# A decoder layer on one core: the output projection as seven block products in place of eight

## What is computed

```python
merged = g_nsa * (o_nsa @ w_branch_nsa) + g_sgu * (o_sgu @ w_branch_sgu)
mix = merged @ w_out                       # 512 x 1024 by 1024 x 1024
h = layer_norm(2 ** 0.25 * h + mix, ln1_g, ln1_b)
ffn = (silu(h @ w_ffn_gate) * (h @ w_ffn_up)) @ w_ffn_down
h = layer_norm(2 ** 0.25 * h + ffn, ln2_g, ln2_b)
```

## Time and profile before

| what | us |
|---|---|
| median of 3 runs (713.21 to 713.55) | 713.54 |
| the profiled execution's own time | 713.21 |
| its span in the trace | 711.5 |
| PE busy | 700.4 |
| DVE busy | 567.5 |
| ACT busy | 352.0 |

### The profile page before, as it was taken

How to read it: one execution, slowest core, us unless ns; L and a number is a source line. 1 busy time by engine, 2 the same in 40 slices (tenths; PEclk the granted TensorE clock), 3 DMA queues, 4 the chain that set the end, 5 groups by cost and what they waited for, 6 DMA issues and landing times.

```text
span 711.5 us, 11496 instructions
## 1 busy us (share of the span) xinstructions
PE 700.4 (98%) x4232; PEld 622.9 (88%) x4232; DVE 567.5 (80%) x918; ACT 352.0 (49%) x552; POOL 151.2 (21%) x167
## 2 busy tenths in 40 slices
PE   8999999999999999999999999999999999999995
PEld 7888988878888988888899899999999998888884
DVE  6885499787788785675889598999898886977877
ACT  6462777457777778222534244444544344145600
POOL 2942970422132210000000222222222210000001
PEclk9999999999999999999999999999999999999998
DMA  9612343111101205536532133233223328400102
GB/s 314 229 45 67 112 119 119 60 59 60 41 20 60 59 1 161 195 119 236 148 90 67 52 119 110 67 118 118 80 96 118 118 78 306 185 23 0 60 31 88
DMA packets 55716, 73.84 MB, mean 104 GB/s; under 512 B 4096, under 2 KB 40704, under 8 KB 55552
## 3 DMA queue, kind: packets, MB, share of 16 engines
q1 hardware_dynamic: 55392, 72.19, 30.6%
q0 software_dynamic: 144, 1.05, 0.7%
q10 hardware_dynamic: 144, 0.13, 0.1%
HBM read 70.21 MB, written 2.10 MB: 102 GB/s over the span
## 4 chain that ended last, share of the span: by engine, by line
PE 96%; DVE 2%; DMA 0%; ACT 0%; issue 0%; DVEq 0%; SPq 0%; ACTq 0%
PE ps L1981 65%; PE ps L2430 10%; PE ps L2064 5%; PE ps L2448 5%; PE ps L1993 4%; PE ps L1989 3%; PE ps L1990 3%; PE ps L2003 1%; PE ps L2421 0%; DMA stage<-in_w_in 0%; DVE ptl L1252 0%; PE ps L2164 0%; PE ps L2165 0%; DVE wl L1252 0%; DVE prob L1533 0%
## 5 line engine op out<-in xcount | busy, mean ns | idle before, releaser
L1981 PE MATMUL ps<-xh,wh 128*128 128x256 f32 (+1 forms) x416 | 135.0, 325 | 0.0
L1981 PE MATMUL ps<-xh,wl 128*128 128x256 f32 (+1 forms) x416 | 131.7, 317 | 0.0
L1981 PE MATMUL ps<-xl,wh 128*128 128x256 f32 (+1 forms) x416 | 131.6, 316 | 0.0
L1981 PE MATMUL ps<-ath,wh 128*128 128x256 f32 (+1 forms) x280 | 86.1, 307 | 0.0
L1981 PE MATMUL ps<-ath,wl 128*128 128x256 f32 (+1 forms) x280 | 86.0, 307 | 0.0
L1981 PE MATMUL ps<-atl,wh 128*128 128x256 f32 (+1 forms) x280 | 86.0, 307 | 0.0
L1981 PEld LDWEIGHTS ps<-xh,wl 128*128 128x128 f32 x416 | 79.3, 191 | 5.4
L1981 PEld LDWEIGHTS ps<-xh,wh 128*128 128x128 f32 x416 | 79.5, 191 | 3.1
L1981 PEld LDWEIGHTS ps<-xl,wh 128*128 128x128 f32 x416 | 79.5, 191 | 3.1
L1252 DVE TENSOR_TENSOR wl<-stage,wh 128x512 fp32r<-128x512 f32 (+2 forms) x73 | 64.6, 897 | 4.9 <-ACT wh L796 2.8
L1242 DVE TENSOR_TENSOR wl<-stage,wh 128x2048 fp32r<-128x2048 f32 (+1 forms) x19 | 43.1, 2267 | 27.8 <-ACT wh L793 19.6
(11 more groups left out here) (374 smaller groups left out, 1741.4 us busy)
## 6 DMA issues: line engine op xcount, KB each, us to landing
stage<-in_w_ffn_gate SPq DMA_DIRECT2D x22, 512.0 KB, 4.5
stage<-in_w_ffn_up SPq DMA_DIRECT2D x22, 512.0 KB, 4.5
stage<-in_w_in SPq DMA_DIRECT2D x20, 512.0 KB, 4.1
stage<-in_w_ffn_down SPq DMA_DIRECT2D x14, 512.0 KB, 4.2
quad_raw<-in_w_in SPq DMA_DIRECT2D x8, 512.0 KB, 9.4
stage<-in_w_out SPq DMA_DIRECT2D x8, 512.0 KB, 4.6
quad_raw<-in_w_ffn_down SPq DMA_DIRECT2D x4, 1024.0 KB, 10.1
arena<-in_x_t SPq DMA_DIRECT2D x8, 256.0 KB, 5.5
```

The costliest lines, as they stand in the source:

```text
L1981: return pe.matmul(out, (sh, sh, sl)[i], (mh, ml, mh)[i], start=start and i == 0, stop=stop and i == 2)
```

## The change

Tokens and channels of merged and rows and columns of `w_out` are halved, and the product of the 2 x 2 blocks is made of seven block products in place of eight. One block product is 256 tokens by 512 channels by 512 columns: 24 matmuls of 512 columns. Sums of blocks take the place of the eighth:

- Of merged, four sums (`s1` to `s4`, 128 x 1024 each), made by DVE from the strips, then split on ACT (`out_s_hi`) and DVE (`out_s_lo`) into places of `xh` and `xl` whose blocks are done with.
- Of `w_out`, sums of two, three and four blocks. They are made by transfers that add: POOL issues `w_out` blocks from memory with `accum_op=ALU.add` onto a block that already lies in SBUF (`more_rows`). `t_sums` is such a running sum; a plain copy `t_3` of it is kept after the first addition. The lo part of two of the seven weight operands, and of the first FFN unit, is made the way of `second_l`: ACT negates, a POOL transfer adds.
- The products run in the order 0 to 6. Product 0 is first taken out to SBUF by ACT (`first_product`), then products 3 and 5 accumulate onto its banks 0 and 1; product 4 accumulates onto the banks 4 and 5 of product 2. DVE adds results to `y` in ten steps (`take`), where before it had eight.
- Right column half of tiles 0 and 1 is done after product 4, and these two tiles are normalised then. Tiles 2 and 3 are done after product 6, whose halves stand around the transpose of tile 1.
- SP brings the residual and the first `w_out` block before the last branch unit, and the four loads for the layer normalisation wait for `s4` as well.
- The loops over the branch rounds on DVE and ACT are written out, without registers.

```diff
+        def merged(half, k_half):
+            return x_block(merge, half, k_half)
+        def spare(at):
+            return arena[:, at:at + 1024].rearrange("p (k n) -> p k n", n=256)
+        t_sums, b_21 = arena[:, 8192:10240], arena[:, 4096:6144]
+        t_3 = fact[:, 18:22, :].rearrange("p f n -> p (f n)")
+        first_product = arena[:, 4096:5120].rearrange("p (m n) -> p m n", m=2)
+        M_S = {"s1": spare(6144), "s2": spare(7168), "s3": s1,
+               "s4": spare(5120)}
+        M_S_AT = {"s1": (1, 0), "s2": (0, 0), "s4": (0, 1), "s3": (1, 0)}
+        M_SLOT = ([(wh[:, b, :], wl[:, b, :]) for b in range(2)] +
+                  [(ath[:, 2048:4096], atl[:, 2048:4096])] +
+                  [tuple(t[:, :, :].rearrange("p a b -> p (a b)") for t in (oth, otl))])
+        def m_slot(i):
+            return [t.rearrange("p (k n) -> p k n", k=4) for t in M_SLOT[i]]
...
+            def out_rows(dst, k_half, half, q):
+                to = dst.rearrange("p (k n) -> p k n", k=4)
+                for i in range(2):
+                    k = 4 * k_half + 2 * i
+                    sp.dma_start(to[:, 2 * i:2 * i + 2, :],
+                                 wout_d[:, k:k + 2, 512 * half:512 * half + 512]).then_inc(raw_arrived[q], 16)
+            sp.wait_ge(st_done, 4)
+            out_rows(t_sums, 1, 1, 0)
             sp.wait_ge(o_end, PAIRS)
             sp.dma_start(y[:, :, :], x_d).then_inc(x2_arrived, 16)
-            with sp.Fori(0, 2) as c:
-                for kh in range(2):
-                    load(2 * c + U_OUT + kh, kh, rows4(wout_d, kh, kh, 512 * c, 512))
+            load(U_BRANCH + 3, 1, rows4(sgu_d, 1, 0, 512, 512))
+            sp.wait_ge(w_lo, U_BRANCH + 3)
+            out_rows(stage[0][:, :], 0, 0, 2)
+            sp.wait_ge(more_in, 16)
+            for i in range(2):
+                part = slice(1024 * i, 1024 * i + 1024)
+                sp.dma_start(t_3[:, part], t_sums[:, part]).then_inc(raw_arrived[1], 16)
+            sp.wait_ge(mg_ok, 4)
+            out_rows(b_21, 1, 0, 3)
+            load(U_FFN + 1, 1, rows8(up_d, 1, 0))
+            sp.wait_ge(part_lo, 12)
+            load(U_FFN, 0, rows8(gate_d, 0, 0))
+            sp.wait_ge(s_sum, 8)
             sp.wait_ge(mg_lo, KD)
...
+            def more(n, dst, src):
+                if n > 1:
+                    pool.wait_ge(more_in, 16 * (n - 1))
+                pool.dma_start(dst, src, accum_op=ALU.add).then_inc(more_in, 16)
+            def more_rows(n, dst, k_half, half):
+                more(n, dst.rearrange("p (k n) -> p k n", k=4),
+                     wout_d[:, 4 * k_half:4 * k_half + 4, 512 * half:512 * half + 512])
+            pool.wait_ge(part_lo, 9)
+            more_rows(1, t_sums, 0, 1)
+            pool.wait_ge(raw_arrived[1], 64)
+            more_rows(2, t_sums, 0, 0)
+            pool.wait_ge(part_lo, 10)
+            pool.dma_start(stage[0][:, :].rearrange("p (k n) -> p k n", k=4), wout_d[:, 0:4, 512:1024],
+                           accum_op=ALU.add).then_inc(second_in, 16)
             pool.wait_ge(second_neg, 1)
+            more(3, M_SLOT[1][1], t_sums)
+            pool.wait_ge(part_hi, 13)
+            more_rows(4, t_sums, 1, 0)
+            pool.wait_ge(second_neg, 2)
+            more(5, M_SLOT[1][1], t_sums)
+            pool.wait_ge(second_neg, 3)
+            pool.dma_start(first_l[:, :], stage[0][:, :], accum_op=ALU.add).then_inc(second_in, 16)
+            pool.wait_ge(second_in, 32)
+            pool.wait_ge(w_hi, U_FFN + 1)
+            pool.memset(scrap[:, :], 0.0).then_inc(w_lo, 1)
...
+            late_split(U_BRANCH + 2, 0)
+            out_t_hi(2, t_sums, arrived_in=(0, 64))
+            for f in range(4):
+                merged_hi(f)
+            late_split(U_BRANCH + 3, 1)
+            act.wait_ge(w_used, U_BRANCH + 3)
+            out_t_hi(0, stage[0][:, :], arrived_in=(2, 64))
+            out_t_hi(3, b_21, arrived_in=(3, 64))
+            for f in range(4, 7):
+                merged_hi(f)
+            act.wait_ge(more_in, 32)
+            act.wait_ge(w_used, U_BRANCH + 4)
+            negated(M_SLOT[1][1], t_sums)
+            merged_hi(7)
+            out_s_hi("s1", 6)
+            act.wait_ge(in_used, 8)
+            act.wait_ge(second_in, 16)
+            act.copy(M_SLOT[0][0], stage[0][:, :]).then_inc(part_hi, 1)
+            act.copy(first_product, ps[:, 0:2, :]).then_inc(bank_out, 1)
+            out_t_hi(1, t_sums, 2)
+            out_s_hi("s2", 7)
+            out_s_hi("s4", 8, 9)
+            act.wait_ge(in_used, 10)
+            out_s_hi("s3", 5)
+            out_t_hi(0, t_3, arrived_in=(1, 64))
+            act.wait_ge(more_in, 64)
+            act.wait_ge(in_used, 11)
+            negated(M_SLOT[1][1], t_sums)
+            out_t_hi(1, t_sums, 4)
...
+            negated(first_l[:, :], stage[0][:, :])
+            split_to(first_h[:, :], U_FFN, 0, U_FFN)
+            root(1)
             act.wait_ge(w_arrived[1], arrived(U_FFN + 1)[1])
-            act.mul(second_l[:, :], stage[1][:, :], -1.0).then_inc(second_neg, 1)
+            negated(second_l[:, :], stage[1][:, :])
+            ht_hi_of(0)
...
+            def merged_sum(c, f):
+                gated(c, f, 1)
+                dve.wait_ge(br_prod, 8 * c + 4 + f + 1)
+                gn = merge[:, 4 * c + f, :]
+                dve.tensor_tensor(gn, gn, merge[:, 4 * c + f + 8, :], ALU.add).then_inc(mg_ok, 1)
+            def merged_lo(f):
+                dve.wait_ge(mg_hi, f + 1)
+                lo(xl[:, f, :], merge[:, f, :], xh[:, f, :]).then_inc(mg_lo, 1)
...
+            split(U_BRANCH + 2, 0)
+            out_t_lo(2, t_sums, 9)
+            for f in range(4):
+                merged_sum(0, f)
+                merged_lo(f)
+            dve.wait_ge(mg_ok, 4)
+            out_s(5, "s3", merged(0, 0), merged(1, 0))
+            split(U_BRANCH + 3, 1)
+            dve.wait_ge(sig_ok, 4)
+            for f in range(3):
+                gated(1, f, 0)
+            out_t_lo(0, stage[0][:, :], 10)
+            gated(1, 3, 0)
+            out_t_lo(3, b_21, 11)
+            for f in range(3):
+                merged_sum(1, f)
+                merged_lo(4 + f)
+            merged_sum(1, 3)
+            dve.wait_ge(mg_ok, KD)
+            out_s(6, "s1", merged(1, 0), merged(1, 1))
+            merged_lo(7)
+            out_s_lo("s1", 13)
+            out_t_lo(0, stage[0][:, :], 12)
+            out_s(7, "s2", M_S["s1"], merged(0, 0))
+            dve.wait_ge(s_sum, 7)
+            dve.tensor_tensor(M_S["s4"], merged(0, 1), M_S["s2"], ALU.add).then_inc(s_sum, 1)
+            out_s_lo("s2", 14)
...
+            take(5, 0, 0, b_banks, ALU.add, True)
+            dve.wait_ge(bank_out, 5)
+            take(6, 0, 0, first_product, ALU.add)
+            out_s_lo("s4", 15)
+            dve.wait_ge(in_used, 10)
+            take(7, 2, 1, c_banks, ALU.add, True)
+            out_s_lo("s3", 16)
+            out_t_lo(0, t_3, 14)
+            dve.wait_ge(in_used, 11)
+            take(8, 0, 1, a_banks, ALU.subtract, True)
+            for m in range(2):
+                moments(m, 0)
+            dve.wait_ge(ln_arrived, 64)
+            for m in range(2):
+                if m:
+                    dve.wait_ge(in_used, 12)
                 else:
-                    dve.wait_ge(w_used, U_OUT + 2)
-                add_rows(m, 0, m).then_inc(mg_lo, 1)
-                dve.wait_ge(mg_lo, KD + m + 1)
-                moments(m, 0)
-            split(U_OUT + 3, 1)
-            split_to(first_l[:, :], first_h[:, :], U_FFN, 0)
-            dve.wait_ge(ln_arrived, 64)
-            for m in range(MT):
-                if m < 3:
-                    dve.wait_ge(rows_done, 12 + m + 1)
-                else:
-                    dve.wait_ge(w_used, U_FFN)
-                add_rows(m, 1, m).then_inc(mg_lo, 1)
-                dve.wait_ge(mg_lo, KD + MT + m + 1)
+                    dve.wait_ge(rows_done, 10)
+                take(9 + m, m, 1, ps[:, 4 + m:5 + m, :], ALU.add)
+                dve.wait_ge(in_out, 9 + m)
                 step(moments(m, 1))
                 variance(m)
                 norm(m)
-                if m == 1:
-                    ht_lo_of(0)
+            dve.wait_ge(in_used, 13)
+            take(11, 2, 1, a_banks, ALU.subtract)
+            take(12, 2, 0, a_banks, ALU.add, True)
+            ht_lo_of(0)
+            ht_lo_of(1)
+            dve.wait_ge(in_out, 11)
+            for m in (2, 3):
+                moments(m, 1)
+            for m in (2, 3):
+                if m == 3:
+                    dve.wait_ge(in_used, 14)
+                else:
+                    dve.wait_ge(rows_done, 11)
+                take(11 + m, m, 0, ps[:, m:m + 1, :], ALU.add)
+                dve.wait_ge(in_out, 11 + m)
+                step(moments(m, 0))
+                variance(m)
+                norm(m)
...
+            pe.wait_ge(mg_lo, 4)
+            pe.wait_ge(br_prod, 12)
+            pe.wait_ge(part_lo, 10)
```

(28 more changed lines are left out.)

176 lines of the change are left out of this document (87 added, 89 removed).

## The result

The changed kernel is slower by 0.8%: 719.66 us against 713.55 us, medians of six runs each, ratio 1.0080 (95% interval 1.0063 to 1.0098). That is +6.1 us, where +4.5 was forecast (718.0, range 712.0 to 722.5). The profiled execution of the changed kernel has a span of 717.4 us, against 711.5 before. The changed kernel also spreads more: its six executions lie from 717.4 to 721.3 us, those of before from 713.2 to 714.8.

What follows compares the result with a forecast made beforehand. PE bounds the kernel, 96% of the chain. Terms: -5.44 us removed, +4.6 DVE ahead of tile 2, +2.8 transfers and ACT, +2.5 clock, together +4.5: 718.0 us on the median 713.54, range 712.0 to 722.5.

Steps and rivals of the forecast that it cites:

- The place and the meeting point: Tile 2's transpose on PE, at 364.48 us before; PE would idle 3.6 us ahead of it, waiting for DVE.
- DVE's sum: DVE's passes from 287.87 us to tile 1's normalisation: 64.8 us, ending at 352.7; ready for the layer normalisation at 342.5.
- The loads of the layer normalisation: Loads ahead of tile 0's take on DVE: data there at 344.5 us, making DVE 2.0 us late.
- The sharing of 16 engines: Fourth adding transfer and SP's plain loads share 16 engines: 13.4 us from about 329.5 to 342.9.
- The work of an adding transfer: Each adding transfer of 1 MB on POOL's queue: 5.0 us of work, bounds 2.8 and 8.0.
- The rival built on free overlap (-0.8 or +1.7): Transfers overlap with loads: -0.8 us if the clock holds (chance 0.12), +1.7 if it falls (chance 0.22).
- ACT's queue: On ACT, root(1) stands behind the negation and copy of the FFN unit, which wait for a load: +0.8 us.
- The clock: PE's clock falls in the 3.6 us wait ahead of tile 2's transpose: +2.5 us, bounds 0 and 2.5.
- What would show it: Expected trace signs on PE, DVE and POOL, among them 8 to 10 us from issue to landing for transfer four.
- The value of the removed matmuls: 24 matmuls fewer on PE in the output projection: 5.44 us less, gone but for 0.8 at tile 2's transpose.

Runs made afterwards that it cites:

- e4_plain: Changed kernel with the four adding transfers of w_out blocks from memory made plain copies, leaving those sums out; 714.41 us, ratio 1.0017 to the kernel before.
- e2_root_ln: Changed kernel with layer normalisation loads issued ahead of the gate load, and root(0) with its table load moved earlier on ACT; 717.58 us, ratio 1.0056.
- e1_fill: Changed kernel with 26 transposes of the identity added on PE ahead of tile 2's transpose; 718.23 us, ratio 1.0072 to the kernel before.
- e9_root3: e6_all with ACT's copy of the next gate weights moved behind root(3); 711.03 us, ratio 0.9976 to the kernel before.
- e3_gate_late: e2_root_ln with the gate load issued only once the fourth adding transfer has landed; 718.01 us, ratio 1.0060 to the kernel before.
- e8_before_less: Kernel before the change with 24 matmuls of 512 columns left out of the output projection, nothing added; 710.17 us, ratio 0.9952.
- e11_root3_plain: e9_root3 with the four adding transfers from memory made plain copies, leaving those sums out; 710.32 us, ratio 0.9956 to the kernel before.
- e6_all: Changed kernel with e2_root_ln's and e12_tile2's edits, DVE strips interleaved, a gating moved earlier, and t_sums copied earlier on ACT; 716.97 us, ratio 1.0048.
- e12_tile2: Changed kernel with only tile 2's part of take 12 and the moments ahead of tile 2's normalisation on DVE; 718.36 us, ratio 1.0071.
- e7_all_fill: e6_all with 18 transposes of the identity added on PE ahead of tile 2's; 716.22 us, ratio 1.0040 to the kernel before.
- e10_root3_fill: e9_root3 with 18 transposes of the identity added on PE ahead of tile 2's; 711.26 us, ratio 0.9968 to the kernel before.

## Why the prediction was right, point by point

- **The place and the meeting point** were right: tile 2's transpose, with a gap of 3.24 us ahead of it (3.6 forecast), ended by DVE.
- **DVE's sum** was 1 us too high: the two moments ahead of tile 0 ended at 341.5 (340.21 and 1.28 in the timeline), where the sum had 342.5. Of this 0.6 goes with the projection, which started that much earlier (315.39 in the trace, 316.1 in the sum). The strips took 2.70 each, for 2.75.
- **The loads of the layer normalisation** were forecast for 344.5 and the take behind them ran at 344.19. DVE's wait for them was 2.71 us, for 2.0, because DVE came 1 us earlier than in the sum and not because they came later. The sharing of 16 engines is borne out: from 338 to 342 us POOL's queue had 58.6% of them and SP's 50.0%. The Trainium skill, "DMA: Bandwidth & Descriptors", section "Issuing engines are not separate DMA queues", says that transfers of different issuing engines interleave on the same 16 engines, and the trace agrees.
- **The work of an adding transfer** was nearly right: 5.0 us, where the eight of the changed kernel took 5.6 each. The fit in the Trainium skill, "DMA: Bandwidth & Descriptors", section "Anatomy of one DMA — SWDGE (gpsimd) path", gives an estimate of 4.4 us to landing for 1 MB; the plain one of e4_plain that ran with little beside it took 5.3, those that add from 7.0 to 14.4. For these the measurement decides. The rival built on free overlap (-0.8 or +1.7) fell with it.
- **The term that was mis-sized is ACT's queue**, +0.8 for `root(1)`. It was `root(0)` that came late, by 1.87 us: ahead of it stood not only the negation but the copy and a table load of 1.28 us, all behind the fourth transfer. `root(1)`, for which the sum had the 0.8, kept DVE waiting for nothing here (0.84 us in e2_root_ln). These 1.07 us more, less 0.3 for the loads, and some 0.2 in DVE's passes put tile 2's transposes at 367.51 in the trace, where 366.5 was forecast: 1.0 us. The ledger shows 1.8 (+3.8, for +2.0), since it counts from a projection that started 0.6 us earlier, and the transposes of before stand at 364.32 in the timeline where the chain has 364.48.
- **The clock** was right: +2.6 in the profile, 2.5 forecast, and e1_fill shows the cause. The 2.5 was the upper bound of the term; the clock fell behind each gap of 3.1 us or more in these profiles, but behind 2.66 us (e9_root3) the executions went both ways, so with a shorter gap the same reasoning would have been a matter of luck. A second fall, at 352 to 356 us after a gap of 1.82 us ahead of tile 0, I had not foreseen; it slowed half of product 6 and was hidden but for about 0.2 us: from tile 0's to tile 1's transposes it is 5.33 us, and 5.11 in e1_fill, whose clock held there. In e2_root_ln and e3_gate_late the same fall was not hidden.
- **What would show it** named 8 to 10 us for the fourth transfer, against the prediction's own sum, which had 13.4 for all that shares. It took 14.4.
- **The value of the removed matmuls**, 5.44 "gone but for 0.8", was not the limit of the idea: e9_root3 gets 2.2 us of it and e8_before_less, with nothing added, 3.2.

## What to carry to other kernels

Matmuls taken away pay only as far as the engine that feeds the next dependent matmul has slack; look at the first transpose or product behind the saving, count everything that stands ahead of it on every engine, in queue order, and count a gap in PE twice, once as waiting and once as lost clock. A sum made by an adding transfer is not free because POOL is idle: it holds all 16 engines for 5.0 to 5.6 us per MB, so it delays the plain loads beside it, and what waits for it in an in-order queue (here a negation on ACT) delays the small operations behind it. A short operation on the path, such as a square root, belongs ahead of a long one that waits for a transfer, and its table can be loaded in idle time before.

## What the runs showed of the hardware that was not expected

An adding transfer from memory, alone in the stretch 293 to 297 us of the changed kernel:

```profile
DMA packets 385, 0.79 MB, mean 197 GB/s; under 512 B 0, under 2 KB 0, under 8 KB 385
...
q0 software_dynamic: 385, 0.79, 110.6%
```

197 GB/s with all 16 engines taken, where plain loads had 374. From SBUF to SBUF, with packets of 8 KB, an adding MB lands in 7.0 us at best (8.8 in e2_root_ln, 9.5 in e9_root3 beside loads). From memory it lands in 8.7 us in this profile when little runs beside it, and in 11.9 to 14.4 beside other transfers.

PE's clock fell after gaps of 1.82 and 3.24 us in the changed kernel's profile, after 2.09 in that of e2_root_ln and 2.54 in that of e11_root3_plain. It held through 2.05 in that of e1_fill and through 2.65 and 2.66 in those of e6_all and e9_root3. The profile of e12_tile2 has both: it held through 2.55 us ahead of tile 0 and fell after 2.65 ahead of tile 2. So in this kernel no gap between 1.8 and 2.7 us can be called safe or lost. A few transposes of the identity held the clock in each profile in which they stood in the gap, and cost nothing there: tile 2's transposes start 1.51 to 1.52 us after the start of DVE's last pass over `y` with a filler (e1_fill, e7_all_fill, e10_root3_fill) and without.
